# Attention's queries and keys turned around three conditioning chunks at the end of a state-space scan

## The reference, cut to what matters

```python
m = (jax.nn.silu(cvec) @ w_mod + b_mod)             # adaln: 12 chunks of 512 per layer
y = y.reshape(...)                                  # the scan's sum, both directions
y = rmsnorm(y * jax.nn.silu(z), ssd_norm)           # gated output
ql = axial_rope(rmsnorm(q), row, col)               # queries and keys, already finished
kl = axial_rope(rmsnorm(k), row, col)               # before the scan starts
s = einsum(q, k) * scale; p = exp(s - max); o = p @ v / denom
out = concatenate([y, o], axis=-1) @ w_out
```

## Time and profile before

| what | us |
|---|---|
| median of three runs | 1268.35 |
| the three runs | 1266.33 to 1270.63 |
| the profiled execution, whole | 1270.54 |
| its span in the trace | 1268.7 |
| from the first output chunk's rows to the first exponential | 224.13 to 246.07 |

### The profile page before, as it was taken

The page is one execution under the profiler, slowest core; times in us unless marked ns, Lnnn a source line. Parts: engine busy times, 40 slices in busy tenths (PEclk is TensorE's granted clock), DMA queues, the critical chain, the costliest instruction groups (busy, mean ns, idle before and its releaser), DMA issues.

```text
span 1268.7 us, 13672 instructions
## 1 busy us (share of the span) xinstructions
PE 1089.1 (86%) x5217; PEld 577.3 (46%) x5233; DVE 488.2 (38%) x889; ACT 239.2 (19%) x449; POOL 234.0 (18%) x235
## 2 busy tenths in 40 slices
PE   3799989799976999999993999998768579979992
PEld 0446456466443544444551644445543345534441
DVE  0436669452034222212326683335632423322212
ACT  2223123564032000000014321110011101100001
POOL 0201023000113533323013020000001444431001
PEclk8899989999986999999996999998758689999997
DMA  9723159704435799998989432130057379999972
GB/s 347 249 69 133 66 185 333 278 2 172 160 133 219 293 415 413 412 415 331 413 341 373 167 118 78 67 133 1 1 215 314 109 297 413 410 415 417 422 322 114
DMA packets 72862, 309.79 MB, mean 244 GB/s; under 512 B 10286, under 2 KB 12526, under 8 KB 55628
## 3 DMA queue, kind: packets, MB, share of 16 engines
q1 hardware_dynamic: 61627, 291.10, 58.7%
q0 software_dynamic: 10288, 14.37, 3.3%
q10 hardware_dynamic: 864, 3.15, 0.6%
HBM read 308.41 MB, written 15.34 MB: 255 GB/s over the span
## 4 chain that ended last, share of the span: by engine, by line
PE 70%; DMA 12%; DVE 8%; ACT 3%; issue 3%; another core or an unknown queue 1%; SPq 1%; POOL 1%; ACTq 0%; DVEq 0%; POOLq 0%
DMA ring<-in_moe_w 9%; PE psum L1961 9%; PE psum L1958 8%; PE psum L1319 8%; PE psum L1224 7%; PE psum L1993 6%; PE psum L591 5%; PE psum L1988 4%; PE psum L583 3%; PE psum L411 3%; PE psum L1332 2%; PE psum L1570 1%; PE psum L1569 1%; PE psum L901 1%; PE psum L1104 1%
## 5 line engine op out<-in xcount | busy, mean ns | idle before, releaser
L2074 POOL DMA_INDIRECT arena<-hdram,idxl x128 | 129.0, 1008 | 269.8 <-DVE arena L2033 175.4
L2048 DVE TENSOR_TENSOR arena<-arena,psum 128x512 f32<-128x512 f32 x32 | 22.0, 688 | 287.3 <-PE psum L1961 130.4
L1319 PE MATMUL psum<-arena,ring 128*128 128x512 f32 (+1 forms) x256 | 97.8, 539 | 0.0
L1224 PE MATMUL psum<-ring,arena 128*128 128x512 f32 x192 | 85.3, 607 | 1.5 <-ACT arena L1209 1.5
L411 PE MATMUL psum<-ring,spad 128*32 128x512 f32 x384 | 59.1, 744 | 27.5 <-DMA ring<-in_w_mod 20.7
L1958 PE MATMUL psum<-ring,arena 128*64 128x256 f32 x608 | 70.6, 388 | 11.6 <-DVE arena L2033 8.3
L1248 POOL TENSOR_TENSOR wide<-wide,arena 128x512 f32<-128x512 f32 x12 | 15.2, 1268 | 349.5 <-DVE arena L1237 349.5
L1958 PE MATMUL psum<-arena 128*64 128x256 f32 x672 | 77.6, 388 | 1.1 <-issue 1.1
L1961 PE MATMUL psum<-arena 128*128 128x512 f32 x160 | 69.9, 594 | 1.6 <-DMA arena<-in_moe_w 1.6
L2016 ACT ACTIVATE arena<-psum 128x512 f32<-128x512 f32 x32 | 19.1, 598 | 274.2 <-PE psum L1988 166.3
L591 PE MATMUL psum<-ring,arena 128*128 128x512 f32 (+1 forms) x192 | 69.0, 522 | 0.0
(11 more groups left out here) (387 smaller groups left out, 1523.0 us busy)
## 6 DMA issues: line engine op xcount, KB each, us to landing
ring<-in_moe_w SPq DMA_DIRECT2D x46, 2048.0 KB
arena<-in_moe_w SPq DMA_DIRECT2D x45, 2048.0 KB
ring<-in_w_mod SPq DMA_DIRECT2D x24, 2048.0 KB
ring<-in_od_w_in SPq DMA_DIRECT2D x6, 2048.0 KB
wide<-in_moe_w SPq DMA_DIRECT2D x5, 2048.0 KB
ring<-in_ev_w_in SPq DMA_DIRECT2D x3, 2048.0 KB
arena<-ydram SPq DMA_DIRECT2D x6, 1024.0 KB, 7.0
ring<-in_ev_w_out SPq DMA_DIRECT2D x2, 2048.0 KB
```

The source lines that it names most:

```text
L1224: mm = pe.matmul(bank(n % 6), catT[:, k, P * t:P * t + P], w[:, k, :], start=k == 0, stop=k == KD - 1)
L1319: mm = pe.matmul(bank(bk, tok.stop - tok.start), w[:, k, P * (b % 4):P * (b % 4) + P], hT[:, k, tok], start=k == 0, stop=k == KD - 1)
L2074: pool.indirect_dma_start(xq[e % NX][:, 256 * g:256 * g + 256], None, xrows(l), bass.IndirectOffsetOnAxis(ap=idxl[:, g, e:e + 1], axis=0), ...
```

## The change

The doubling of the keys on VectorE moves to the scan's end, ahead of `diagonal(7)`, and no longer waits for the transposes of the gated outputs. TensorE turns tiles 0 and 1 of queries and keys ahead of chunk 12's rows and tiles 2 and 3 between chunk 12's rows and its columns. ScalarE copies tiles 0 and 1 out ahead of its first square, tiles 2 and 3 ahead of its second. The gated outputs are turned into banks 4 to 7 in place of 0 to 3, inside `pe_att`, after the scores of the first two pairs. `qT` and `kT2` move to the place of `xbcT`, which the scan has then read. The number of instructions on each engine is the same; no DMA is moved.

```diff
-    qT = view(4096, [4, TOK])
-    kT2 = view(6144, [2, TOK])
+    qT = view(8192, [4, TOK])
+    kT2 = view(10240, [2, TOK])
@@ dve_ssd
             dve_mod(SSD_MOD0[i])
+        dve_att_prepare()
         diagonal(7)
@@ act_ssd_out
         for t in range(NT):
+            if t < 2:
+                for u in (2 * t, 2 * t + 1):
+                    act_att_turned(u)
             act.wait_ge(*act_more("yz_ready"))
@@ pe_ssd_out
         pe.wait_ge(*pe_more("arg_ready", 2))
-        pe.wait_ge(S("ydiag_done"), 8)
-        pe.wait_ge(S("yoff_done"), 6)
-        for m in OUT_MODS:
-            pe_mod(m)
+        pe.wait_ge(*pe_more("qk_ready"))
+        pe_att_turn(0)
+        pe.wait_ge(S("ydiag_done"), 7)
+        pe.wait_ge(S("yoff_done"), 6)
+        pe_att_turn(1)
+        pe_mod_rows(OUT_MODS[0])
+        for t in (2, 3):
+            pe.wait_ge(*pe_more("qkT_ready"))
+            pe_att_turn(t)
+        pe_mod_cols(OUT_MODS[0])
+        for m in OUT_MODS[1:]:
+            pe_mod(m)
+        pe.wait_ge(*pe_more("qkT_ready", 2))
+
+        pe.wait_ge(S("ydiag_done"), 8)
+        pe.wait_ge(S("mcol_done"), OUT_MODS[2] + 1)
@@ dve_att_prepare
-        dve.wait_ge(S("cat_full"), NT)
@@ pe_att
             if p < PAIRS:
                 scores(p)
+            if p == 1:
+                pe_ssd_cat()
```

More of the change, by code:

```diff
@@ L998, in act_ssd_out @@
             act.wait_ge(*act_more("cat_full"))
-            act.activation(catT[:, 0:4, P * t:P * t + P], bank(t).rearrange("p (b n) -> p b n", b=4), ACT.Copy
+            act.activation(catT[:, 0:4, P * t:P * t + P], bank(4 + t).rearrange("p (b n) -> p b n", b=4), ACT.Copy
                            ).then_inc(S("cat_act"), 1)
@@ L1003, in pe_ssd_out, with pe_ssd_cat @@
         pe.wait_ge(*pe_more("arg_ready", 2))
+        pe.wait_ge(*pe_more("qk_ready"))
[11 more added lines that the diff above has]
+        pe.wait_ge(*pe_more("qkT_ready", 2))
         pe.wait_ge(S("ydiag_done"), 8)
-        pe.wait_ge(S("yoff_done"), 6)
-        for m in OUT_MODS:
-            pe_mod(m)
+        pe.wait_ge(S("mcol_done"), OUT_MODS[2] + 1)
+    def pe_ssd_cat():
         for t in range(NT):
@@ L1010, in pe_ssd_out @@
             for b in range(4):
-                mm = pe.transpose(psum[:, t, P * b:P * b + P], ysum[:, t, P * b:P * b + P], ident)
+                mm = pe.transpose(psum[:, 4 + t, P * b:P * b + P], ysum[:, t, P * b:P * b + P], ident)
             mm.then_inc(S("cat_full"), 1)
@@ L1025, in dve_att_prepare, with act_att_turned, pe_att_turn @@
             dve_step(last) if g == 0 else last.then_inc(S("qk_ready"), 1)
[L1027 to L1046, removed]
+    def act_att_turned(t):
+        act.wait_ge(*act_more("qk_full"))
+        b = 2 * (t % 2)
+        act.activation(qT[:, :, P * t:P * t + P], bank(b).rearrange("p (b n) -> p b n", b=4), ACT.Copy)
+        act.activation(kT2[:, :, P * t:P * t + P], bank(b + 1, 256).rearrange("p (b n) -> p b n", b=2), ACT.Copy
+                       ).then_inc(S("qkT_ready"), 1)
+    def pe_att_turn(t):
+        b0 = 2 * (t % 2)
+        for b in range(4):
+            pe.transpose(psum[:, b0, P * b:P * b + P], qkv[:, t, P * b:P * b + P], ident)
+        for b in range(2):
+            mm = pe.transpose(psum[:, b0 + 1, P * b:P * b + P], kdup[:, t, 2 * b:2 * b + 2, :].rearrange("p a n -> p (a n)"), ident)
+        mm.then_inc(S("qk_full"), 1)
     def nkeys(t):
@@ L2400, in _ @@
             act_ssd_out()
-            act_att_prepare()
             act_att()
@@ L2451, in _ @@
             dve_ssd_out()
-            dve_att_prepare()
             dve_att()
@@ L2504, in _ @@
             pe_ssd_out()
-            pe_att_prepare()
             pe_att()
```

## The result

The changed kernel is slower: 1275.03 us against 1267.82, ratio 1.0047 with a 95% interval of 1.0032 to 1.0063, 6.0 us by the ratio, 7.2 by the medians. The changed kernel's single times fall in two groups, twelve at 1272.6 to 1279.3 and two at 1264.3 and 1265.0, with the profiled one at 1270.3 between them; one execution four times as long was disturbed and is left out. Timed again later it had 1273.75, ratio 1.0056 (1.0038 to 1.0075).

The account below looks back on a forecast made before the run. TensorE, busy 86% of the span, was taken to bound the kernel. 5.89 us gained less 2.29 lost gave 3.60, less 0.9 for the clock 2.7, so 1265.6 against a median of 1268.35; range 1262.3 to 1269.7.

Parts of the forecast that it names:

- Part 1 and 2: Doubled keys ahead of the sum, off the path; two query and key tiles delay chunk 12's rows 1.62 us.
- Part 3: Two query and key tiles inside chunk 12: its columns 0.67 us later, so the scaling starts 2.29 later in all.
- Part 4: From the scaling to the first exponential: 5.39 us in place of 11.28, a gain of 5.89, table load last.
- Sum at full clock: Up to the first exponential: 5.89 us gained less 2.29 lost, 3.60 us earlier, before any cost of the clock.
- The clock: Idle time behind the last gated tile: one fall of some 3.2 us over the first pairs, costing 0.9 us.
- Rival S: Pairs with 256 keys: clock falls in the idle time and stays down, 4.6 us slower, 1273; chance 0.08.
- I count the gain whole: Behind the first exponential: the gain there reaches the kernel's end, as the next weights' loads move with attention.
- strong form: TensorE's moved transposes: the skill's rule that transposes do not engage the full clock, taken as rival C.
- rival C: Chunks 13 and 14: transposes do not hold the clock, a loss of about 0.8 us, 1269.2; chance 0.10.

Follow-up runs that it names:

- the filled: Changed kernel plus two useless 128x512 matmuls on TensorE in the idle stretch before the first probabilities: 1265.24 against 1266.54 us for the kernel before, ratio 0.9997.
- table version: Changed kernel with the exponential's table loaded early by a dummy exponential behind chunk 14's copy: 1263.53 against 1266.54 us for the kernel before, ratio 0.9974.
- old order with a gap: Kernel before plus four useless copies on ScalarE ahead of the exponential's table load: 1283.35 against 1266.54 us for the kernel before, ratio 1.0138.
- gated outputs first: Changed kernel with the gated outputs turned ahead of the first two pairs' scores: 1263.47 against 1268.23 us for the kernel before, ratio 0.9959.

## Why the prediction was wrong

Forecast 1265.6, range 1262.3 to 1269.7; measured 1275.0.

- Part 1 and 2, two tiles ahead of chunk 12: its rows expected 1.62 later against the scan. Measured 224.85 - 222.29 = 2.56 behind the last reduction, before 0.89: 1.67. Right. The copy on ScalarE was not late: it had been idle for 0.30.
- Part 3: 2.29 to the scaling expected. Measured 13.75 behind the last reduction against 11.55: 2.20. Right. The two other chunks kept their pace: 3.58 and 3.65 from reduction to reduction, in both kernels.
- Part 4: 5.39 from the scaling to the first exponential; measured 5.39 (236.04 to 241.43), released by the table load and not by the maximum (ready at 239.6). Right. Sum at full clock 3.60 against 3.69; the terms came out one by one, so this part was not luck.
- The clock: here it failed. I expected the fall in this idle stretch, and it came there. But I let it last "one stretch of some 3.2 us", from the one fall whose length show, and priced it at 0.9 us. It lasted 24 us and cost 8.6, and a second fall cost 1.45. What I had not asked is what brings the clock back. In the old trace it returned at 239.4 (0.79 over the microsecond from 239), 3.4 us behind its fall, while TensorE did 16 transposes and then idled, and I took the pairs of heads as denser than those. With the clock down a pair takes 3.80 us and spreads the same matmuls over that time. The run with three dense matmuls shows that work of another kind brings it back within 1.5 us.
- Rival S named this mechanism, its place and its price a pair ("up to 2.05 more", measured 1.75) and the sum came out at 1273; I gave it 0.08. The argument against it was the one just told.
- "I count the gain whole": up to the projection rightly so, since the filled and the table version keep theirs until there. To the end it is shown in part: the table version has 3.3 of 3.94 us, the filled one 0.4. The loss goes through. The gate rows at 1.2 GHz, 1.45 us, I had not foreseen as a second place.
- The rule of the Trainium skill weighed there ("TensorE: Matmul & The Clock Gate", section "Part 4: PE-mode transpose": transposes do not count as busy in the way matmuls do) I set aside on the strong form. With transposes beside the chunks the clock stayed at 1.00 from 223 to 241, so rival C is out. Whether the transposes inside the pairs are part of why the clock stayed down, no run here tells.

The old trace had the answer to what the clock does over small matmuls, further on. In the second layer the clock fell at 877.7 and stayed down for 17 us, while TensorE was busy, mostly with small matmuls (L1569, L1570) for 13.23 of the 14 us from 880:

```profile
876.00:878.00 2.00, 1.14 (x5) 0.93 0.00 0
880.00:894.00 14.00, 13.23 (x54) 0.50 0.00 0
894.00:896.00 2.00, 1.63 (x14) 0.80 0.00 0
```

Two bf16 matmuls of 128x512 stood inside that time and did not end it:

```profile
880.15 1.04 PE L1545 MATMUL psum<-cb 128*128 128x512 bf16 x2
```

Spread over the pairs, a fall as long as this one costs some 8 us (17 us hold 4.5 pairs of 3.80, each 1.75 longer; an estimate from these rows), which is rival S's price.

## What to carry to other kernels

When a reordering shortens a chain, look at where the engine with the clock is left idle afterwards, and what it does next: a gap of 2.65 us in front of small dependent matmuls cost more than twice what the whole reordering gained (8.63 against 3.69 us). Price a fall of the clock by what follows until dense work returns, not by the last fall seen, and look for the longest fall in the trace at hand. Such a gap is cheap to close: move a table load out of it, split it with ready work, or put two large matmuls without use in it; and look at PEclk before the busy share, which reads full at half rate.

## What the runs showed of the hardware

- At 1.2 GHz a pair of 256 keys took 3.80 us and not 2.05; the clock was down for 24 us in the changed kernel (twice) and 27 us in the old order with a gap, though PE read as busy throughout. Three float32 matmuls of 128x512 ended it; two bf16 ones of that size, in a fall of 17 us in the second layer of the kernel before, did not. What ended it without them is open: in one trace it came back at 265.5, ahead of the first pair with 512 keys, in the other at 280.4, inside it.
- Idle pieces of 0.69 and 0.99 us with 1.1 us of matmuls between them, and one of 1.23 us, left the clock up where 2.65 us brought it down. The length of one piece is not all of it: in the old order the clock also fell just behind the start of the gated outputs' transposes, ahead of which TensorE had idled 0.72 and 1.01 us (the kernel before at 236.0, and the runs with other places and with a gap); with 0.72 and 1.10 us there it did not (gated outputs first). Ahead of the gate rows the same two pieces went either way in ten traces. What decides there, no run tells.
- Useless work made the kernel faster: two matmuls in a gap were worth 10.3 us on the stretch against the same kernel without them, and 6 us of the whole time by the ratios.
- Places in SBUF and PSUM banks of the moved blocks had no effect that shows (91.49 against 91.44 us on the stretch, ratio 0.996 to 1.0006).
